# Modulation sums of the opening regrouped into blocks of four k-tiles by 512 columns, and later ones put behind other units, in a two-block transformer kernel

## The reference, cut to what matters

```python
ada = (c @ w_ada + b_ada)[:, None, :]          # c: 1 x 1024, w_ada: 1024 x 6144
shift1, scale1, gate1, shift2, scale2, gate2 = jnp.split(ada, 6, axis=-1)
h = rmsnorm(x, g_norm1) * (1.0 + scale1) + shift1
proj = h @ w_in                                # 1024 x 5452, cut into q, k, v, indexer, gates
y_fox = forgetting_attention(q_f, k_f, v_f, cumsum(log_sigmoid(f_logit + b_forget)))
y_dsa = indexer_sparse_attention(q_d, k_d, v_d, q_i, k_i, w_i, rel_bias)   # top 64 keys by an indexer
merged = sigmoid(gate_fox) * (y_fox @ w_branch_fox) + sigmoid(gate_dsa) * (y_dsa @ w_branch_dsa)
x = x + gate1 * (merged @ w_out)
h2 = rmsnorm(x, g_norm2) * (1.0 + scale2) + shift2
x = x + gate2 * (square(relu(h2 @ w_mlp1)) @ w_mlp2)
```

## Time and profile before

| | us |
|---|---|
| median of 3 runs (range) | 1117.15 (1115.64 to 1118.68) |
| the profiled execution | 1116.6 |
| its span, first to last instruction | 1114.8 |
| PE busy | 1067.2 |
| DVE, ACT, POOL busy | 644.7, 545.5, 373.9 |

### The profile page before, as it was taken

How to read it: one execution, slowest core, us unless ns; L and a number is a source line. 1 busy time by engine, 2 the same in 40 slices (tenths; PEclk the granted TensorE clock), 3 DMA queues, 4 the chain that set the end, 5 groups by cost and what they waited for, 6 DMA issues and landing times.

```text
span 1114.8 us, 19839 instructions
## 1 busy us (share of the span) xinstructions
PE 1067.2 (96%) x8566; PEld 1046.3 (94%) x8566; DVE 644.7 (58%) x834; ACT 545.5 (49%) x770; POOL 373.9 (34%) x198
## 2 busy tenths in 40 slices
PE   6889999999999999989999999999999989999998
PEld 6889999999999999989999999999998779999998
DVE  3857756665775554635855454445857656544443
ACT  3357866633556434563335354443754544443341
POOL 2436257231464532452021352222331411352221
PEclk9989999999899999999999999999999999999999
DMA  9987748536377555524355555556533215655541
GB/s 324 288 269 234 221 126 293 187 115 190 112 256 260 177 178 189 189 96 133 114 189 190 189 189 189 180 179 200 154 121 100 77 45 183 227 177 176 178 151 39
DMA packets 173957, 197.39 MB, mean 177 GB/s; under 512 B 5380, under 2 KB 146093, under 8 KB 173741
## 3 DMA queue, kind: packets, MB, share of 16 engines
q1 hardware_dynamic: 173868, 196.11, 54.5%
HBM read 195.03 MB, written 1.06 MB: 176 GB/s over the span
## 4 chain that ended last, share of the span: by engine, by line
PE 83%; DVE 5%; ACT 3%; POOL 2%; DMA 2%; issue 2%; SPq 2%; DVEq 1%; ACTq 0%; POOLq 0%
PE bank L502 82%; DMA ada_raw<-in_w_ada 2%; DVE w_lo L1743 1%; ACT w_hi L1185 1%; SPq L458 1%; POOL ada_raw L1593 1%; DMA probsT<-in_buckets 1%; POOL stat L1705 1%; ACT ada_raw L1175 1%; PE bank L757 0%; POOL head_bias L1628 0%; DVE y_tok L2285 0%; DVE big L2154 0%; ACT h_hi L1222 0%; ACT big L1234 0%
## 5 line engine op out<-in xcount | busy, mean ns | idle before, releaser
L1743 DVE TENSOR_TENSOR w_lo<-w_raw,w_hi 128x2048 fp32r<-128x2048 f32 x158 | 385.8, 2445 | 244.7 <-ACT w_hi L1185 243.6
L502 PE MATMUL bank<-h_hi,w_hi 128*128 128x256 f32 x1328 | 378.7, 290 | 11.8 <-DVE w_lo L1743 7.6
L502 PE MATMUL bank<-h_hi,w_lo 128*128 128x256 f32 x1328 | 373.4, 286 | 0.0
L1185 ACT ACTIVATE w_hi<-w_raw 128x2048 fp32r<-128x2048 f32 x158 | 301.4, 1909 | 129.3 <-PE bank L502 121.6
L502 PE MATMUL bank<-h_lo,w_hi 128*128 128x256 f32 x1328 | 347.8, 285 | 1.2 <-POOL h_lo L1561 1.2
L502 PE MATMUL bank<-u_hi,w_hi 128*128 128x256 f32 x1024 | 290.9, 287 | 4.1 <-ACT u_hi L1194 2.7
L502 PE MATMUL bank<-u_hi,w_lo 128*128 128x256 f32 x1024 | 288.6, 285 | 0.0
L1561 POOL TENSOR_TENSOR u_lo<-fresh,u_hi 128x512 fp32r<-128x512 f32 x60 | 142.4, 2375 | 402.1 <-ACT u_hi L1194 402.0
L502 PE MATMUL bank<-u_lo,w_hi 128*128 128x256 f32 x1024 | 277.1, 284 | 0.0
L502 PEld LDWEIGHTS bank<-h_hi,w_hi 128*128 128x128 f32 x1328 | 259.9, 196 | 17.5 <-DVE w_lo L1743 9.4
L502 PEld LDWEIGHTS bank<-h_hi,w_lo 128*128 128x128 f32 x1328 | 259.8, 196 | 0.0
(11 more groups left out here) (247 smaller groups left out, 1023.1 us busy)
## 6 DMA issues: line engine op xcount, KB each, us to landing
w_raw<-in_w_mlp SPq DMA_DIRECT2D x32, 1024.0 KB, 5.4
w_raw<-in_w_up SPq DMA_DIRECT2D x32, 1024.0 KB, 5.4
w_raw<-in_w_down SPq DMA_DIRECT2D x32, 1024.0 KB, 5.1
w_raw<-in_w_in SPq DMA_DIRECT2D x21, 1024.0 KB, 6.0
ada_raw<-in_w_ada SPq DMA_DIRECT2D x19, 1024.0 KB, 7.9
w_raw<-in_a_w_in SPq DMA_DIRECT2D x10, 1024.0 KB, 5.2
w_raw<-in_w_o SPq DMA_DIRECT2D x8, 1024.0 KB, 5.0
w_raw<-in_w_out SPq DMA_DIRECT2D x4, 1024.0 KB, 4.9
```

Source lines behind the costliest of these rows:

```text
L502: return pe.matmul(dst, lhsT, rhs, start=start, stop=stop, skip_group_check=True)
L1185: act.activation(w_hi[:, n % PARTS_RING, :], w_raw[:, slot_of[n], :], ACT.Copy).then_inc(hi_w, 1)
L1743: dve.tensor_tensor(w_lo[:, n % PARTS_RING, :], w_raw[:, slot_of[n], :], w_hi[:, n % PARTS_RING, :].bitcast(F32), ALU.subtract).then_inc(l ...
```

## The change

- a0 to a7 become blocks of 4 k-tiles (512 rows) by 512 columns: a(2j) and a(2j+1) are the two halves of the rows of the same 512 columns. DVE takes a0, a1, a2, a4, a6, a7 (four steps of 512 columns each; a1 and a7 go on in the sum of a0 and a6). ACT scales a3 and POOL adds it. PE takes a5 with `c` as weights and 512 moving columns (`ada_rows`), ACT copies that row. PE adds the parts over the partitions in `ada_block`. `ada_direct` is gone.
- The sum of squares of x is made by one ACT instruction and three POOL adds in place of 4 squares and 32 one-column matmuls.
- The queue: the small tables come ahead of the constants; w0 is loaded ahead of a6 and a7; the load of `mem` moves from behind w4 to behind w18.
- DVE splits w0 ahead of a6 and a7, not behind the bias.
- PE issues `keep_busy` matmuls (128x512, float32, their result unused): five behind block 2, two behind block 3.
- Unit 0 has an order of its own (`first_unit`): all 32 products with `h_hi` follow the arrival of its quarters, then 16 with `h_lo`; two quarters of `h_lo` are made by POOL and two by DVE; four buffers replace the ring of two; ACT's split of w1 comes behind all of `h_hi`.
- `ADA_LATE` carries a8 to a13 with units 4, 6, 8, 10, 11, 12; a14 on stay at 14, 16, ... ACT scales a8 behind the indexer's scores and a9 behind the evacuation of unit 4.
- On POOL the first attention's mask follows a8; a9 to a14 are summed ahead of the second attention's bias, then come a15, the two `u_lo` splits, and a16 to a19.

```diff
-ADA_LATE = {**{2 + 2 * i: ADA_FIRST + i for i in range(12)}, **{32 + 4 * i: 20 + i for i in range(4)}}
+ADA_LATE = {n: ADA_FIRST + i for i, n in enumerate((4, 6, 8, 10, 11, 12, 14, 16, 18, 20, 22, 24, 32, 36, 40, 44))}
-    early = ["a0", "a1", "a2", "a3", "a4", "a5", "a6", "a7", "w0", "w1", "w2", "w3"]
+    early = ["a0", "a1", "a2", "a3", "a4", "a5", "w0", "a6", "a7", "w1", "w2", "w3"]
...
-            ada_direct(0)
             pe.wait_ge(consts_in, 16)
-            for q in range(4):
-                add_squares(1, q)
+            pe.wait_ge(ada_vector, 2)
+            ada_block(0, ada_part[:, 0, :])
+            sum_x("sum1")
             into_misc("row")
...
-            ada_direct(3)
-            ...
+            ada_rows(5)
             pe.wait_ge(ada_vector, 3)
-            ada_columns(7, ada_part[:, 2, :], ones[:, 0:1])
+            pe.wait_ge(ada_quarter, 1)
+            ada_block(1, ada_part[:, 1, :], other=probs[:, 0, :])
+            pe.wait_ge(ada_vector, 4)
+            pe.wait_ge(ada_copied, 1)
+            ada_block(2, ada_part[:, 0, :], row=ada_row)
+            keep_busy(WARM_A)
+            pe.wait_ge(ada_vector, 6)
+            ada_block(3, ada_part[:, 1, :])
+            keep_busy(WARM_B)
+
+            def first_unit():
+                ...
+                for q in range(4):
+                    pe.wait_ge(h1_hi, q + 1)
+                    pair(q, wh, h_hi, False)
+                    pair(q, wl, h_hi, False)
+                for q in range(4):
+                    pe.wait_ge(*((h1_lo_pool, q + 1) if q < 2 else (h1_lo_vec, q - 1)))
+                    ins = pair(q, wh, h_lo, True)
+                ins.then_inc(unit_done, 1)
...
+            split_w(0)
+            dve.wait_ge(ada_done, 2)
+            ada_unit(6)
             ada_unit(7)
...
-            for a in range(11, 14):
+            for a in range(ADA_FIRST + 1, 15):
                 ada_unit(a)
-            for q in range(2):
-                split_h(J_FOX + q, u_lo, u_hi, 2 * q)
...
-            for a in range(14, 20):
+            ada_unit(15)
+            for q in range(2):
+                split_h(J_FOX + q, u_lo, u_hi, 2 * q)
+            for a in range(16, 20):
                 ada_unit(a)
```

More of the change, by code:

```diff
@@ L46 @@
 RING = 4
+WARM_A, WARM_B = 5, 2
 PARTS_RING = 3
@@ L485, in _ @@
                 .then_inc(bias_in, 16)
-            load(loads[position["w", 4] + 1], ("w", N_M1V))
+            load(loads[position["w", 4] + 1], ("w", N_GD))
+            for half, tile in enumerate((mem_k, mem_v)):
+                sp.dma_start(tile.rearrange("p l a t -> p (l a) t"), mem[:, 4 * half:4 * half + 4, :]).then_inc(mem_in[half], 16)
+            load(loads[position["w", N_GD] + 1], ("w", N_M1V))
             sp.dma_start(flat(big, 6, 9)[:, 0:2 * T + P], tables["rope"]).then_inc(late_in, 16)
@@ L596, in product_tok, with keep_busy, ada_rows @@
                 last.then_inc(unit_done, 1)
-            def ada_direct(a):
+            def keep_busy(times):
+                for _ in range(times):
+                    mm(acc[2][:, :], ident, consts[:, :], True, True)
+            def ada_rows(a):
                 tiles = ada_tiles(a)
@@ L602, in ada_direct, with ada_block @@
                 pe.wait_ge(vec_in, 16)
[L603 to L606, removed]
+                for kt in range(4):
+                    last = mm(acc[1][0:1, :], vec[:, V_C + 4 * (a % 2) + kt:V_C + 4 * (a % 2) + kt + 1],
+                              tiles[:, kt, :], kt == 0, kt == 3)
                 last.then_inc(ada_used, 1)
+            def ada_block(j, part, other=None, row=None):
+                for c in range(4):
+                    at, c0 = ps_ada[:, 4 * j + c:4 * j + c + 1], c * P
+                    last = mm(at, part[:, c0:c0 + P], ones[:, 0:1], True, other is None and row is None)
+                    if other is not None:
+                        last = mm(at, other[:, c0:c0 + P], ones[:, 0:1], False, True)
+                    if row is not None:
+                        last = mm(at, row[:, c0:c0 + P], ones[0:1, 0:1], False, True)
+                last.then_inc(ada_done, 1)
             def ada_columns(a, part, over):
@@ L1267, in _ @@
             act.wait_ge(x_in, 16)
[L1268 to L1271, removed]
+            act.activation(flat(qk, 0, 8), flat(xT, 0, 8), ACT.Square).then_inc(x_squared, 1)
+            for k in range(4):
+                if k == 0:
+                    ada_in(act, 3)
+                    act.wait_ge(vec_in, 16)
+                last = act.activation(ada_tiles(3)[:, k, :], ada_tiles(3)[:, k, :], ACT.Copy, scale=vec[:, V_C + 4 + k:V_C + 5 + k])
+            last.then_inc(ada_quarter_scaled, 1)
             split_w(0)
+            act.wait_ge(ada_used, 1)
+            act.activation(ada_row, acc[1][0:1, :], ACT.Copy).then_inc(ada_copied, 1)
             act.wait_ge(ada_ready, 2)
```

171 lines of the change are left out of this document (94 added, 77 removed).

## The result

| | before | after |
|---|---|---|
| median of 4 runs each (range), us | 1117.87 (1115.64 to 1118.68) | 1100.92 (1100.11 to 1102.20) |
| ratio, 95% interval | | 0.9857 (0.9842 to 0.9873) |
| the profiled execution, us | 1116.6 | 1100.1 |
| its span, us | 1114.8 | 1098.3 |

A forecast was written before the change was run, and what follows sets the result against it. PE, busy 1067.2 of 1114.8 us, was taken to bound the kernel, gaining only from removed waits or higher clock. 1116.6 - 11.0 - 1.5 = 1104.1, median 1104.6; main case 1102 to 1107, 8 in 10 for 1100 to 1111.

The forecast's parts named there:

- the stall behind a8: Before unit 2: PE's 4.4 us wait for ACT, and 2.4 us of low clock after it, would go.
- the opening ahead of `gs`: Loads and sums at the start: `gs` at 42.4 us instead of 43.4, bound by DVE behind w0.
- the order on POOL: Around the second attention: a14's sum no longer waits for the bias pieces, a16 lands earlier, 1.5 us less.
- better: Rival: 2 KB pieces move faster and the short waits at units 8 and 14 vanish, 1101 us; chance 0.08.
- to the end of unit 2: From the start: unit 2 ends at 62.9 us instead of 73.95, 11.0 us less.
- unit 3 to the second attention: Gain kept through the dense units; unit 17's evacuation ready when PE is, 1.5 us less.
- the warm-up stands in the way: Rival at block 3: clock falls, five matmuls end at 46 or 47; 1107 to 1112 us; chance 0.14.
- Unit 0 to unit 2: Products 0.12 us apart, unit 1 from 50.8 after a 1.3 us wait, unit 2 at the high clock.
- a8 to a15: Modulation loads: a8 hidden with 4 us left, a13 slips some 0.3 us, ACT waits for a15 until 164.
- modulation binds ACT in units 9 to 16: Rival: landings take 8 us, three waits each pass 1 to 2 us to PE; 1108 to 1110; chance 0.09.
- the rule of the Trainium skill: DVE instructions with two SBUF inputs and POOL's SBUF reads block each other; 0.6 us at most, not in the sum.

The follow-up runs named there:

- experiment 5: The changed kernel with each block a0 to a7 loaded by two DMAs of 256 columns, in 1 KB pieces: 1104.23 us, ratio 0.989.
- experiment 1: The changed kernel without its seven warm-up matmuls (both sets left out): 1101.43 us, ratio 0.9873 to the kernel before.
- experiment 11: The changed kernel with three warm-up matmuls behind block 2 instead of five and DVE's split of w0 behind a7: 1100.76 us, ratio 0.9859.
- Experiment 2: The changed kernel with a8 back at unit 2, scaled behind the split of w2 as before: 1104.81 us, ratio 0.9901.
- Experiment 4: The kernel before, with only a8's scaling moved behind the evacuation of unit 1: 1110.94 us, ratio 0.9956.
- experiment 3: The changed kernel with POOL's old order for a14, the second bias and the u_lo splits: 1113.81 us, ratio 0.9973.
- experiment 12: The kernel before with POOL's new order alone: 1112.84 us, ratio 0.9972.
- experiment 10: The changed kernel with three warm-up matmuls behind block 2 in place of five: 1101.91 us, ratio 0.9871.
- the control: The changed kernel run once more, unaltered: 1102.2 us, ratio 0.9877 to the kernel before.
- experiment 7: The changed kernel with DVE's split of w0 moved behind a7, ahead of the bias: 1102.58 us, ratio 0.9879.
- experiment 8: The changed kernel with two extra float32 matmuls in PE's 1.46 us wait ahead of unit 24: 1103.54 us, ratio 0.9883.

## Why the prediction was right, and where its sum was off

The forecast for the profiled execution was 1104.1 and it took 1100.1. The path was right: the stall behind a8, the opening ahead of `gs`, the order on POOL. The sum is 4.0 us short, and the result lies 0.9 us inside the lower end of the range, where the prediction had its rival "better" (1101, chance 0.08). Of that rival one half came true, for pieces of 2 KB did load faster; the short waits did not vanish, for two of 0.44 us are left. And 1.5 of the 4.0 us is a stretch of low clock that no run ties to the change, with 0.6 more untraced: that much is luck, and without it the forecast would be 1.9 us off. The 16.5 us by place, from the marks:

| | forecast | measured | from |
|---|---|---|---|
| to the end of unit 2 | 11.0 | 13.2 | 73.95 - 60.79 |
| unit 3 to the second attention | 1.5 | 1.3 | 184.49 - 170.01 = 14.48, less 13.2 |
| from there to 257.80 | 0 | 1.5 | 273.74 - 257.80 = 15.94, less 14.48 |
| the rest | 0 | 0.6 | 16.5 - 15.94 |

**To `gs`: the mechanism right, two terms too large.** The prediction put a5 at 25.2 "as before" and w0 at 4.9 us behind it, both from rows of loads in 1 KB pieces. PE took a5 at 23.87 without a wait for it, and w0 had landed at 27.62, 2.9 us earlier than its 30.5. The rate of 340 to 350 GB/s, which the sum carried over, is that of 1 KB pieces; with 2 KB ones the queue moved 387 (experiment 5). That experiment gives 2.4 us of w0's date back. It has a5 at 26.63, later than the 25.2 of the kernel before at the same rate; where that 1.4 us comes from, the doubled number of DMAs or the order of the small tables, stays open. With w0 early, DVE's split waited for x_hat and not for w0, at 30.55 instead of 32.4, and the sum of a7 ended at 38.85 instead of 40.9: 2.1 us, and the first `h_hi` came 1.7 earlier than forecast. The step sizes were right: four steps forecast at 3.1 us took 3.11, block 3 forecast at 1.0 took 0.95, the split 2.29.

**Which engine binds at block 3.** The forecast said DVE; the runs say PE by 0.4 us and DVE close behind. The prediction's span for PE, ready between 39.5 and 47, held but for 0.2 us at its low end (39.3), and at 44.4 in experiment 5. Why it comes out so long is in the windows of PE after:

```profile
26.00:28.00 2.00, 2.00 (x4) 1.00 1.15 305
...
32.00:34.00 2.00, 2.00 (x11) 0.98 1.09 355
34.00:36.00 2.00, 2.00 (x3) 0.50 1.10 347
38.00:40.00 2.00, 2.00 (x11) 1.00 1.10 354
```

`ada_rows` did raise the clock (its instructions went from 0.85 to 0.43 us apart at 27 us), and the one-column blocks behind it let it fall again. The five matmuls therefore took 6.1 us and not 4.5, and this is what the rival "the warm-up stands in the way" says: in kind it happened, but its price was 0.4 us here and 3.7 in experiment 5. Without any warm-up (experiment 1) the kernel loses only 0.7 us, so the five matmuls are close to worthless where they are; three with the split moved are the better use (experiment 11).

**Unit 0 to unit 2.** The gain grows along the way: 2.7 us at the first `h_hi`, 45.74 - 41.97 = 3.8 at unit 0's first product, 55.15 - 48.97 = 6.2 at unit 1's, 65.47 - 54.82 = 10.7 at the transposes, 13.2 at the end of unit 2. Products came 0.12 us apart from the first on, unit 1 started after 1.01 us of waiting for `w_lo` (forecast 1.3), and no wait for ACT stood ahead of unit 2. Experiment 2 confirms that a8's place counts: 3.8 us with the rest of the change in place. Experiment 4 gives 5.5 us at the end of unit 2 for that move alone in the kernel before, of the 13.2, and 7.1 for the stall and its low clock by themselves.

**a8 to a15.** Hidden, as forecast. ACT waited 0.61 us for a13 (forecast 0.3 us of slip) and 3.55 for a15 (its scaling began at 151.03, which is 164.2 in the times of before; the forecast was 164), and PE lost 0.28 us behind a15 and nothing behind a13. The rival that modulation binds ACT in units 9 to 16 didn't come about. How near it was shows in experiment 3: with POOL late by 13.5 us the same chain cost PE 10.1 us and a low clock behind it.

**Behind the first attention.** 1.5 us forecast, 1.3 measured as the difference of the marks. The forecast had one wait of PE there, which went from 1.50 to 0.44, and so gave 1.1. It overlooked a second one, which the dots of the earlier trace rows stand for: PE waited 0.74 us at 164.68 for DVE's `w_lo`, and 0.28 after. That step was slow in company of POOL, as DVE's line for the split between 140 and 190 us before shows (duration ns min/median/max):

```profile
L1743 DVE TENSOR_TENSOR w_lo<-w_raw,w_hi x8: 2278/2836/6020, 138.4 to 188.1; 128x2048 fp32r<-128x2048 f32 x8
```

POOL was busy for all of 155 to 165 us, with the second bias among other work; no run separates its share. The order alone gives 2.1 in the kernel before (experiment 12) and is worth 11.9 in the changed one (experiment 3). So the size was right for the change as a whole, by two waits and not by one, and the prediction didn't see that the two edits lean on each other: with the dense `ADA_LATE`, the order is a condition and not a gain of its own.

**Contention of DVE and POOL.** DVE's three steps of a2 took 4.44 us for 2.3 elsewhere, beside POOL's adds of the squares, which end at 20.03. This agrees in kind with the rule of the Trainium skill that the prediction weighed, "SBUF — State Buffer", section "Who interferes with whom". That delay ends in a wait of DVE before 22.8 us. A second one doesn't:

```profile
23.30 1.38 DVE L1810 TENSOR_SCALAR v_tok<-w_raw,vec 128x512 f32<-128x512 f32 x1
24.71 3.21 DVE L1812 SCALAR_TENSOR_TENSOR v_tok<-w_raw,vec,v_tok 128x512 f32<-128x512 f32 x3
```

a4's four steps took 27.92 - 23.30 = 4.62 us beside POOL's adds of a3 (22.06 to 25.80), where a7's took 3.11. From there to the end of a7's sum DVE has no gap above 0.19 us, so that x_hat stands about 1.5 us later for it, and the split of w0, whose `w_hi` was ready at 29.53, starts at 30.55: an estimate of 1.0 us on a7's sum, from these rows. The prediction left this out of its sum, with 0.6 us at most; here PE, ready only at 39.34, hid it.

**Not forecast: 1.5 us of clock.** The stretch around the wait of 1.46 us took 40.46 or 40.47 us in three of the fourteen profiles (before, experiments 3 and 10) and 38.97 or 38.98 in the eleven others, kernels of both kinds in both groups. In this pair it fell to the change's favour, but no run ties it to the change. The last 0.6 us lies in such stretches further on, and wasn't traced to a cause; the control's profile differs from the first one by 1.5 us in the same way.

## What to carry to other kernels

Read engines that wait in a fixed order as one chain: a late load that only ACT wants cost PE a wait of 4.4 us at the start, and 2.4 more of low clock behind it, and, where the order on a third engine (POOL) was wrong, 10 us in the middle. Compute the loads' time from the rate at their own piece size, not from the rate of the old layout. Before two edits are priced one by one, ask whether the first uses up the slack on which the second's price rests. And where two engines finish together, speeding up one alone gives nothing (0.1 us and 0.0 in experiments 7 and 10, 1.3 us with both).

## What the hardware showed that was not expected

- The size of the pieces counted above 1 KB: from 14 to 20 us the queue moved 387 GB/s in 2 KB pieces and 348 in 1 KB ones, with one DMA per MB (before) or two (experiment 5) alike.
- PE being 100% busy didn't hold the clock. One-column products let it fall from 1.00 to 0.50 within the two windows 32 to 36 us, in a stretch without any wait; in experiment 5 such products (two instructions each) went from 0.31 to 0.51 us apart at 35 us, in the same way.
- The same wait of 1.46 us was followed by a fall of the clock in 3 of 13 profiles and by none in 10; the fourteenth, experiment 8, had it filled. A profile's microsecond or two behind such a wait can't be put down to an edit.
- Steps of DVE and POOL that ran beside each other were long on both sides: in unit 0 before, POOL's last `h_lo` took 3.24 us and the others 1.39, beside two splits of DVE that took 5.55 together (2.29 alone); in the middle of the kernel a split took up to 6.02 us before and 6.50 after.
